# A hybrid Conformer/S5 layer with routed experts: half of the SSM input moved from the first stage to the second, the upper convolution ahead of quads 4 to 6, and the channel sums of three norms accumulated over tiles in PSUM

## The reference, cut to what matters

```python
def mixer(x, c):
    mod = silu(c) @ w_ada + b_ada       # shift1, scale1, gate1, shift2, scale2, gate2
    h = rms_norm(x, norm1_g) * (1 + scale1) + shift1
    val, gate, u, out_gate = split(h @ w_in, 4)
    z = depthwise_conv(val * sigmoid(gate), conv_w, 31 taps) + conv_b
    y_conv = silu(layer_norm(z, ln_g, ln_b))          # mean and variance over 1024 channels
    s = scan(abar * s + bbar @ u)                     # 64 groups of 16 channels, 64 complex states
    y_ssm = gelu(Re(C s) + D u) * sigmoid(out_gate)
    y = concat(rms_norm(y_conv, g1), rms_norm(y_ssm, g2)) @ w_out
    return x + gate1 * y
def layer(x, c):
    x = mixer(x, c)
    h = rms_norm(x, norm2_g) * (1 + scale2) + shift2
    x = x + gate2 * moe(h)              # top-1 group of 4, top-2 experts of its 8
    return rms_norm(x, final_norm_g)
```

## Time and profile before

| Stage | us from the start | TensorE busy | VectorE busy | granted clock of TensorE | GB/s |
|---|---|---|---|---|---|
| first stage | 0 to 147.45 | 122.94 | 43.46 | 0.92 | 375 |
| second stage | 147.45 to 437.99 | 261.64 | 267.22 | 0.97 | 315 |
| output projection and router | 437.99 to 579.30 | 130.80 | 38.93 | 0.96 | 186 |
| experts | 579.30 to 1560 | 924.64 | 170.16 | 0.99 | 400 |

### The profile page before, as it was taken

How to read it: one execution, slowest core, us unless ns; L and a number is a source line. 1 busy time by engine, 2 the same in 40 slices (tenths; PEclk the granted TensorE clock), 3 DMA queues, 4 the chain that set the end, 5 groups by cost and what they waited for, 6 DMA issues and landing times.

```text
span 1559.8 us, 18926 instructions
## 1 busy us (share of the span) xinstructions
PE 1440.0 (92%) x7448; PEld 665.8 (43%) x7448; DVE 519.8 (33%) x934; ACT 160.0 (10%) x254; POOL 131.0 (8%) x112
## 2 busy tenths in 40 slices
PE   5999999989779979999999999999999999999967
PEld 2667666656534434343343343343343343343322
DVE  4231999999651230121121121111111111111105
ACT  3040100100310211010010010010010010000001
POOL 1000011539000017000000000000000000000000
PEclk9799999999989989999999999999999999999989
DMA  9999988979646437999999999999999999999991
GB/s 319 388 391 409 356 307 311 389 284 389 219 168 236 145 126 289 422 421 421 421 422 422 421 423 422 422 422 422 422 421 422 421 423 421 423 421 422 422 420 75
DMA packets 108961, 565.47 MB, mean 363 GB/s; under 512 B 10632, under 2 KB 10816, under 8 KB 50608
## 3 DMA queue, kind: packets, MB, share of 16 engines
q1 hardware_dynamic: 105984, 559.98, 89.2%
q10 hardware_dynamic: 2928, 4.81, 1.0%
HBM read 562.62 MB, written 2.13 MB: 362 GB/s over the span
## 4 chain that ended last, share of the span: by engine, by line
PE 62%; DVE 13%; DMA 11%; issue 7%; PEld 4%; PEldq 1%; SPq 1%; ACT 1%; POOL 0%; DVEq 0%; ACTq 0%
PE ps L918 20%; PE ps L952 15%; DMA ring<-in_exp_w_down 10%; PE ps L890 7%; PE ps L972 6%; PE ps L722 3%; DVE arena L1668 3%; PE ps L563 3%; DVE arena L1635 2%; PEld ps L811 2%; PE ps L508 2%; DMA ring<-in_w_ada 1%; PE ps L707 1%; PE ps L524 1%; DVE arena L1623 1%
## 5 line engine op out<-in xcount | busy, mean ns | idle before, releaser
L918 PE MATMUL ps<-ring,arena 128*64 128x512 f32 x2048 | 458.4, 594 | 11.3 <-DMA ring<-in_exp_w_up 7.7
L918 PEld LDWEIGHTS ps<-ring,arena 128*64 128x64 f32 x2048 | 154.6, 137 | 287.9 <-issue 285.9
L952 PE MATMUL ps<-ring,arena 128*64 128x512 f32 x1024 | 242.9, 600 | 26.8 <-issue 13.9
L722 PE MATMUL ps<-arena,ring 128*128 128x256 f32 x768 | 174.5, 386 | 0.4
L722 PEld LDWEIGHTS ps<-arena,ring 128*128 128x128 f32 x768 | 146.0, 192 | 36.8 <-issue 17.2
L952 PEld LDWEIGHTS ps<-ring,arena 128*64 128x64 f32 x1024 | 72.2, 137 | 167.0 <-issue 158.7
L1875 DVE TENSOR_TENSOR arena<-arena,ps 128x512 f32<-128x512 f32 x72 | 49.6, 689 | 277.5 <-PE ps L972 262.8
L890 PE MATMUL ps<-arena 128*64 128x256 f32 x1024 | 123.7, 386 | 6.4 <-issue 3.8
L811 PE MATMUL ps<-ring,arena 128*128 128x512 f32 x256 | 114.1, 605 | 5.8 <-DVE arena L1699 5.7
L1849 DVE TENSOR_SCALAR arena<-ps,mod 128x256 f32<-128x256 f32 x64 | 34.8, 544 | 228.4 <-PE ps L890 228.4
L972 PE MATMUL ps<-arena 128*64 128x512 f32 x448 | 106.5, 595 | 2.9 <-issue 1.9
(11 more groups left out here) (262 smaller groups left out, 747.1 us busy)
## 6 DMA issues: line engine op xcount, KB each, us to landing
ring<-in_exp_w_gate SPq DMA_DIRECT2D x128, 1024.0 KB, 19.7
ring<-in_exp_w_up SPq DMA_DIRECT2D x128, 1024.0 KB, 18.7
ring<-in_exp_w_down SPq DMA_DIRECT2D x128, 1024.0 KB, 22.5
ring<-in_w_ada SPq DMA_DIRECT2D x96, 1024.0 KB, 9.0
ring<-in_w_in SPq DMA_DIRECT2D x32, 1024.0 KB, 11.9
ring<-in_w_out SPq DMA_DIRECT2D x16, 1024.0 KB, 11.6
arena<-in_x SPq DMA_DIRECT2D x2, 1024.0 KB, 7.0
arena<-in_x SPq DMA_DIRECT2D x1, 2048.0 KB, 10.4
```

Source lines behind the costliest of these rows:

```text
L722: last = mm(ps[:, j // 2, (j % 2) * T:(j % 2 + 1) * T], ring[:, s, kk * N + j * P:kk * N + (j + 1) * P], hT[:, k, :], start=(k == 0 and j ...
L918: last = mm(ps[64 * x:64 * x + 64, stage, :], xT[:, k, slot:slot + SLOTS], ring[:, s, kk * N:(kk + 1) * N], start=(k == 0), stop=(k == KD ...
L952: last = mm(ps[half, 2 + n, :], hidT[pr][:, u, half], ring[:, (m + x) % RING, n * N:(n + 1) * N], start=(u == 0), stop=(u == 3), skip_grou ...
```

## The change

Of the 1024 SSM input columns the first stage now computes only the lower 512 (four units of 4 rows x 512 columns in place of eight of 2 rows x 1024); the upper 512 become a chunk of the second stage. The first stage has 36 units, the second 92 in 28 steps. Steps 0 to 19 have one or two modulation units, steps 20 to 27 four or five. VectorE does the upper convolution after quad 3, then quads 4 to 6, the lower convolution and the norms of the convolution branch, and then quad 7 in one piece. `add_tiles` and its semaphore are gone: `channel_sum` is eight matmuls that accumulate in PSUM, straight from `conv` or the squares, and ScalarE squares in two halves. The writes of `scale2` and `shift2` to HBM and back move from ScalarE's queue to SyncE's, between loads of `w_out`. The last read and the fourth sum stand two and two units later in the output projection.

```diff
-A_UNITS, B_UNITS, C_UNITS, D_UNITS = 40, 88, 16, 48
+A_UNITS, B_UNITS, C_UNITS, D_UNITS = 36, 92, 16, 48
...
-U_BANKS = [2, 0, 1, 3]
+U_BANKS = [2, 3]
-CHUNKS = [(1536, "gate", 4), (512, "value", 0), (1024, "gate", 0), (0, "value", 0), (3072, "out_gate", 0), (3584, "out_gate", 4)]
+CHUNKS = [(1536, "gate", 4), (512, "value", 0), (2560, "u", 4), (1024, "gate", 0), (0, "value", 0),
+          (3072, "out_gate", 0), (3584, "out_gate", 4)]
-STEPS_B = 24
+STEPS_B = 28
 def ada_in_step(g):
-    return 3 if g % 3 else 2
+    if g < 20:
+        return 2 if g % 2 else 1
+    return 5 if g in (25, 26) else 4
-DRIVE_AT = [0, 1, 4, 7, 10, 13, 27, 29]
-READ_AT = [3, 7, 9, 13, 15, 29, 32, 49]
-SUM_AT = [42, 44, 47]
+DRIVE_AT = [0, 3, 6, 9, 25, 28, 31, 35]
+READ_AT = [5, 9, 13, 17, 31, 35, 38, 58]
+SUM_AT = [49, 51, 54]
...
@@ SyncE, in the loop over the units of w_out @@
                     sp.dma_start(x1, a["x"][0].rearrange("(t p) d -> p t d", p=P)).then_inc(x_again, 16)
+                    sp.wait_ge(parts_ready, 3)
+                    for i, part in enumerate((4, 3)):
+                        sp.dma_start(col(ab_dram[i]), mod[:, part, :]).then_inc(ab_stored, 16)
+                if m == 9:
+                    sp.wait_ge(ab_stored, 32)
+                    sp.wait_ge(z_ready, 2)
+                    sp.dma_start(ab_rows, ab_dram.rearrange("i (k p) -> (i k) p", p=P)).then_inc(ab_landed, 16)
...
@@ TensorE, channel_sum @@
-                pe.wait_ge(reduced, n + 1)
+                if n == 0:
+                    pe.wait_ge(conv_step, CT_ * TAPS)
...
-                mm(ps[:, 3 if n < 3 else 7, 0:T], mean_w, csum, start=True, stop=True).then_inc(sums, 1)
+                for c in range(CT_):
+                    if n and c % 4 == 0:
+                        pe.wait_ge(squares, 2 * (n - 1) + c // 4 + 1)
+                    last = mm(ps[:, 3 if n < 3 else 7, 0:T], mean_w, (sq if n else conv)[:, c, :], start=(c == 0), stop=(c == CT_ - 1))
+                last.then_inc(sums, 1)
...
@@ TensorE, output projection @@
             out_units([0])
-            side(49)
             out_units([1, 2])
+            side(58)
+            out_units([3, 4])
             channel_sum(3)
-            out_units([3, 4])
+            out_units([5, 6, 7])
             pe.wait_ge(ab_landed, 16)
             tr(ps[:, 6, 0:2 * KD], ab_rows, 2 * KD).then_inc(ab_turned, 1)
-            out_units(range(5, 10))
+            out_units([8, 9])
...
@@ GpSimd @@
             for q in range(4):
                 diagonal(q)
+            z_tiles(1)
+            diagonal(4)
             columns(0)
-            diagonal(4)
-            z_tiles(1)
             diagonal(5)
-            columns(1)
             diagonal(6)
+            diagonal(7)
             z_tiles(0)
             pool.wait_ge(z_ready, 2)
             gp_.memset(mean_w, 1.0 / CH).then_inc(sum_consts, 1)
-            diagonal(7)
+            columns(1)
             columns(2)
             columns(3)
...
@@ VectorE @@
-            for q in range(5):
+            for q in range(4):
                 quad(q)
-
             convolve(1, 0)
-            quad(5)
-            quad(6)
+            for q in range(4, 7):
+                quad(q)
             convolve(0, 1)
-            dve.wait_ge(sum_consts, 1)
-            dve.wait_ge(conv_step, CT_ * TAPS)
-            add_tiles(conv)
             centre()
-            add_squares(1)
             scale_conv()
-
-            def finish_conv():
-                add_squares(2)
-                norm_conv()
-
-            quad(7, finish_conv)
+            norm_conv()
+            quad(7)
...
-            dve.wait_ge(squares, 3)
-            add_tiles(sq)
```

More of the change, by code:

```diff
@@ L565, in tiles @@
                     return last
[L567 to L569 removed]
+                if b == 3:
+                    for pair in range(2):
+                        for kk in range(4):
                             last = tiles(pair, kk)
[L571 removed]
+                        if pair == 0:
                             last.then_inc(chunk_done, 1)
@@ L575, in u_unit @@
                 else:
-                    for kk in range(2):
-                        for pair in range(4):
+                    for kk in range(4):
+                        for pair in range(2):
                             last = tiles(pair, kk)
@@ L663, in _ @@
             columns(1)
-            for n in range(8, 14):
+            for n in range(8, 13):
                 a_unit(n)
@@ L677, in _ @@
             turn_blocks(5)
-            for n in range(18, 21):
+            for n in range(17, 20):
                 a_unit(n)
             turn_blocks(6)
-            for n in range(21, 24):
+            for n in range(20, 22):
                 a_unit(n)
```

86 lines of the change are left out of this document (33 added, 53 removed).

## The result

The changed kernel takes 1546.15 us in the median of 4 runs (1545.94 to 1548.87), against 1560.66 for the kernel before (4 runs, 1559.72 to 1563.14): a ratio of 0.9909, 95% interval 0.9891 to 0.9926. It is faster by 14.5 us. The prediction, 1565.5 us within 1552.5 to 1572, was wrong in sign and in range. The profiled execution took 1545.95 us with a span of 1544.1; before it was 1561.5 and 1559.8, so 15.7 us of span have to be found.

The account below looks back on a forecast made before the run. TensorE was taken to set both stages' length. Output projection start +4.1 us, its first unit -2.5, fourth sum +3.0 gave +4.6: 1566.1 from the profiled 1561.5, 1565.4 for the median; predicted 1565.5, range 1552.5 to 1572.

Parts of the forecast that it names:

- First stage: First stage: ends at 127.3 us, 20 us earlier, with a 5.5 us TensorE wait for ScalarE's fifth column copy, restart 2.5.
- The bound by the transfers: First stage: unit 34's load arrives at 112 us, TensorE wants it at 115, so loads are 3 us from binding.
- T: Second stage: moment the lower gate and value are ready, forecast 201.2 us after the first stage's end.
- Up to the lower convolution: Second stage: upper convolution starts 84.65 us after the first stage, fold costs 1.5 us, TensorE waits 1 to 2 at slot 38.
- The fold of the second part: GpSimd's fold, mostly held until the lower convolution ends: TensorE waits 9.4 us in step 24, plus 2.5 of slow restart.
- P: Start of the output projection: 437.99 us before, forecast at 442.1, or T + 113.6.
- The two held rows: Profile before: GpSimd instructions issued at 280.89 and 341.23 held to the convolution's end, 17.46 and 45.00 us.
- the fold gets its turn: Rival: GpSimd's fold gets in between convolution instructions or wholly before them, 9.4 + 2.5 us go, 1553.6 us; chance 0.17.
- From the sums to the output projection: Second stage's end: norm chain fits behind other TensorE work, cover 3.4 us; output projection's first unit at full clock, -2.5.
- are gone without a gain: VectorE's reductions for the channel sums, 3.6 us each: removing them gains nothing, since they are not last any more.
- A shift of the output projection's start shifts the end one to one: Output projection to the end: everything up to the router is serial ahead of the experts, start forecast +4.1 us.
- the change does all it says: Rival: no wait in the first stage (8.4 us off) or for the fold (11.9 off), 1545 us; chance 0.05.

Follow-up runs that it names:

- experiment 7: Changed kernel with ScalarE's fifth column copy and last transposed store (`keep_read(7)`) moved ahead of the first sine: 1548.15 us, ratio 0.9927.
- experiment 12: Kernel of experiment 11 with the fifth and sixth column copies and `keep_read(7)` ahead of the first sine on ScalarE: 1537.1 us, ratio 0.9844.
- experiment 1: Changed kernel with GpSimd's second fold waiting for the 40th instruction of the lower convolution: 1558.38 us, ratio 0.999.
- experiment 3: Changed kernel with GpSimd's second fold released at the first instruction of the lower convolution's run of 120 (count 4): 1547.2 us, one run.
- experiment 2: Changed kernel with four small GpSimd additions, 16 to 128 columns wide, released inside the upper convolution: 1550.6 us, one run.
- experiment 5: Changed kernel with GpSimd's second fold released after six instructions of the lower convolution's run of 120 (count 10): 1557.2 us, one run.
- experiment 4: Changed kernel with GpSimd's second fold released after two instructions of the lower convolution's run of 120 (count 6): 1560.4 us, one run.
- experiment 8: Kernel before with the channel sums as eight accumulating matmuls on TensorE, otherwise the old order: 1552.79 us, ratio 0.9957.
- experiment 9: Kernel before with the scale and shift vectors' stores and row load moved from ScalarE's queue to SyncE's: 1552.48 us, ratio 0.9961.
- experiment 6: Changed kernel with the channel sums back on VectorE (`add_tiles` and one matmul per sum): 1543.45 us, ratio 0.9887.
- experiment 11: Kernel of experiment 6 with the four tiny router matmuls of experiment 10 added: 1537.94 us, ratio 0.9863.
- experiment 10: Kernel before with four more copies of a tiny router matmul ahead of the experts: median 2.6 us shorter.

## Why the prediction was wrong, by its own steps

In the profiled span the forecast was +4.6 us, the measurement -15.7: 20.3 us apart.

**First stage: right.** End at 127.2 for 127.3, wait 5.4 for 5.5, restart 2.7 for 2.5. The bound by the transfers is there too: in experiments 7 and 12, where TensorE comes 6 to 7 us earlier, loads are late by 1.2 to 1.6 us. (E is the end of the first stage, T the point named above, as in the prediction.)

**Up to the lower convolution: 3.3 us too long.** The upper convolution starts at 210.1, E + 82.9 for E + 84.65; the fold that runs behind it, beside quad 4, costs VectorE nothing (quad 4 begins at the convolution's end, the three quads take 56.5 us as forecast) for the 1.5 us taken; TensorE's waits for the quads, forecast at 1 to 2 us at slot 38, are 0.4. T is 325.2 instead of 328.5.

**The fold of the second part: the step that failed.** The prediction said that "one or two instructions of the fold slip in while VectorE does its four tensor_scalars", the rest only after the convolution, and put 9.4 + 2.5 us on it. All of it passed in 4.1 us, and TensorE waited 0.75 us for 9.4. The first sum ends at T + 59.0 instead of T + 70.8 (-11.8), and P follows at T + 101.4 instead of T + 113.6 (-12.2). The price of the mechanism was right (experiment 1: 12.0 us), its reach was not. The two held rows were both asked inside a run, the later one 3.1 us behind the run's start at 338.15, and I took a fold that begins ahead of the run for the same case: what doesn't fit before the run was to be held, and it passed inside it. The rival named "the fold gets its turn" had this case at 0.17, against the rows.

The rule of the Trainium skill (SBUF — State Buffer, section "SBUF: two separate sides"), an exclusion of one instruction's length, would have given the right sign here; the trace agrees where the fold starts ahead of the run or at its first instruction (experiment 3: a VectorE instruction of 1.28 us beside GpSimd's of 1.23, and then by turns), and not where it asks later (34.10, 41.19, 45.98 and 47.56 us in experiments 1, 2, 5 and 4). The measurement decides: both happen.

**From the sums to the output projection: right.** The two holes of about 6 us and their restarts go, as forecast. Experiments 8 and 9 show what they hung on: the first one on ScalarE's wait of 19.65 us for a DMA or on the reductions (removing either closes it; both together were not run), the second, as it stays in both, most likely on the place of the last sum, which only the new order moves; that was not run alone. The sums on TensorE are no part of the gain in the new order. Back on VectorE they bring 4.9 us from E to P (experiments 6 and 11 alike) and 3 us at the fourth sum; with 0.4 us of an earlier E and less 0.9 for the four small matmuls that is 7.4 of the 7.6 us between the spans of the changed kernel and experiment 11 (8.2 between the medians). The prediction said that the reductions "are gone without a gain"; it did not say that their undoing would pay.

**Experts: 4.7 us not foreseen.** "A shift of the output projection's start shifts the end one to one" is wrong here by the two-piece pause of 5.4 us. Experiment 10 shows that it depends on where the instructions lie, or on the four small matmuls themselves, which stand some 900 us ahead of it; that both the order of work and the pause differ between two kernels makes it look like a gain of the change.

In sum: -12.2 (T to P), -3.3 (up to T), -0.2 (P to the first gather) and -4.7 (experts) are -20.4 of the -20.3. Without the shorter pause the change is worth about 10 us, an estimate: 14.5 less the experts' 4.7. Without the early fold too it would be slower by 1 to 3 us, again an estimate: experiment 1, with the fold held and the short pause, is 1.35 us faster than before, and the short pause is worth 2.6 us (the median of experiment 10) to 4.7. The rival "the change does all it says" (1545, chance 0.05) came within 1.2 us, but by luck: the first stage's 8 us were paid, and 3.3 us up to T and 4.7 at the jump, which it did not have, were won.

## What to carry to other kernels

When GpSimd and VectorE exclude each other, ask at which moment GpSimd asks, not only how long it is held: issued ahead of a long run of VectorE instructions or with its first one, seven dependent instructions got through in 4 us; asked one microsecond later, the first of them took 47 (one run). Sums over tiles belong to the engine that has room after the reordering: the same matmuls won 5.5 us up to the output projection where VectorE's reduction was in the path (experiment 8), and cost 4.9 where TensorE had become full (experiments 6 and 11). Before a small difference is put down to a change, look at every pause on "issue" behind a jump, since an unrelated edit moves it by 5 us.

## What the runs showed of the hardware

- **Held for the run, not the instruction.** A GpSimd instruction asked for inside VectorE's run of 120 scalar_tensor_tensor ended within 1 us of the run's end: 17.46 and 45.00 us (before), 42.20 (changed), 34.10, 41.19 (of 128x16), 47.56 and 45.98 us (experiments 1, 2, 4 and 5).
